# Turning the residual stream on TensorE instead of through DRAM, and scaling it earlier, in a two-block transformer kernel

## The reference

```python
def first_block(x, ...):
    ...
        h = h + jnp.einsum("bsf,fd->bsd", jax.nn.silu(gate) * val, w_down[l])
    return rms_norm(h, final_norm)

def hybrid_layer(x, norm_gain, w_in, w_out, rel_bias, cos, sin):
    hn = rms_norm_2(x, norm_gain)
    proj = hn @ w_in.astype(hn.dtype)
    ...                                  # chunked attention ya (8 heads), retention yr (4 heads)
    y = jnp.concatenate([ya * jax.nn.silu(ag), yr * jax.nn.silu(rg)], axis=-1)
    return x + y @ w_out.astype(x.dtype)

def second_block(x, positions, norm_gain, w_in, w_out, rel_bias, final_gain):
    cos, sin = rotary_tables(positions, RET_HEAD_DIM)
    for layer in range(DEPTH_2):
        x = hybrid_layer(x, norm_gain[layer], w_in[layer], w_out[layer], rel_bias[layer], cos, sin)
    return rms_norm_2(x, final_gain)
```

## Time and profile before

| | us |
|---|---|
| median of 3 runs (1199.81 to 1199.93) | 1199.88 |
| the profiled execution | 1199.93 |
| its span | 1198.1 |
| PE busy | 1187.1 |
| DVE busy | 868.2 |
| ACT busy | 582.3 |
| POOL busy | 286.3 |

### The profile page before, as it was taken

How to read it: one execution, slowest core, us unless ns; L and a number is a source line. 1 busy time by engine, 2 the same in 40 slices (tenths; PEclk the granted TensorE clock), 3 DMA queues, 4 the chain that set the end, 5 groups by cost and what they waited for, 6 DMA issues and landing times.

```text
span 1198.1 us, 15692 instructions
## 1 busy us (share of the span) xinstructions
PE 1187.1 (99%) x5869; PEld 1007.4 (84%) x5869; DVE 868.2 (72%) x1433; ACT 582.3 (49%) x1040; POOL 286.3 (24%) x299
## 2 busy tenths in 40 slices
PE   8999999999999999999999999999999999999998
PEld 7888888888888888888888889889888889899886
DVE  6789755555776487547776788898847788988746
ACT  6666433333443244325444477754445477754542
POOL 0220399921100000000004511266322311012300
PEclk9999999999999999999999999999999999999999
DMA  6421333333331533243333366752223376663621
GB/s 187 132 80 57 97 103 88 105 89 106 124 92 53 153 89 105 72 123 88 105 89 89 105 193 185 201 160 71 71 71 106 96 212 192 179 174 115 159 71 71
DMA packets 213009, 139.53 MB, mean 116 GB/s; under 512 B 5610, under 2 KB 204740, under 8 KB 212804
## 3 DMA queue, kind: packets, MB, share of 16 engines
q1 hardware_dynamic: 212932, 138.52, 39.9%
HBM read 123.82 MB, written 14.68 MB: 116 GB/s over the span
## 4 chain that ended last, share of the span: by engine, by line
PE 94%; DVE 2%; ACT 2%; DMA 1%; issue 1%; SPq 0%; POOL 0%; DVEq 0%; ACTq 0%
PE ps L191 93%; PE ps L194 1%; DMA xtm<-in_x_dram 1%; DVE b_pt L164 1%; ACT whi L161 0%; ACT b_p L161 0%; DVE tmp L164 0%; DMA raw<-in_w_in_dram 0%; DVE b_pd L182 0%; DVE wlo L164 0%; SPq L197 0%; DVE xtm L178 0%; ACT x1l L161 0%; ACT h L161 0%; DVE stat L167 0%
## 5 line engine op out<-in xcount | busy, mean ns | idle before, releaser
L161 ACT ACTIVATE whi<-raw 128x1024 fp32r<-128x1024 f32 (+1 forms) x198 | 206.6, 1051 | 306.1 <-PE ps L191 295.4
L164 DVE TENSOR_TENSOR wlo<-raw,whi 128x1024 fp32r<-128x1024 f32 (+1 forms) x192 | 246.1, 1288 | 48.4 <-ACT whi L161 47.8
L191 PE MATMUL ps<-x0l,whi 128*128 128x512 f32 x1008 | 255.3, 391 | 0.0
L191 PE MATMUL ps<-x0h,whi 128*128 128x512 f32 x1008 | 255.0, 391 | 0.0
L191 PE MATMUL ps<-x0h,wlo 128*128 128x512 f32 x1008 | 253.9, 390 | 0.0
L191 PEld LDWEIGHTS ps<-x0h,wlo 128*128 128x128 f32 x1008 | 188.5, 188 | 38.8
L191 PEld LDWEIGHTS ps<-x0l,whi 128*128 128x128 f32 x1008 | 187.8, 188 | 38.1
L191 PEld LDWEIGHTS ps<-x0h,whi 128*128 128x128 f32 x1008 | 187.5, 188 | 37.9
L164 POOL TENSOR_TENSOR sums<-sums,sq 128x512 f32<-128x512 f32 x28 | 43.6, 1569 | 423.2 <-ACT sq L161 423.2
L191 PE MATMUL ps<-x1h,wlo 128*128 128x512 f32 x304 | 82.3, 389 | 0.0
L191 PE MATMUL ps<-x1h,whi 128*128 128x512 f32 x304 | 82.3, 389 | 0.0
(11 more groups left out here) (190 smaller groups left out, 1671.8 us busy)
## 6 DMA issues: line engine op xcount, KB each, us to landing
raw<-in_w_in_dram SPq DMA_DIRECT2D x98, 512.0 KB, 4.1
raw<-in_w_up_dram SPq DMA_DIRECT2D x44, 512.0 KB, 3.8
raw<-in_w_out_dram SPq DMA_DIRECT2D x24, 512.0 KB, 4.1
turned<-b_pd SPq DMA_DIRECT2D x16, 640.0 KB, 3.2
raw<-in_w_down_dram SPq DMA_DIRECT2D x16, 512.0 KB, 4.1
b_px<-turned SPq DMA_DIRECT2D x32, 160.0 KB, 3.7
b_p<-turned SPq DMA_DIRECT2D x32, 160.0 KB, 3.6
raw<-in_w_down_dram SPq DMA_DIRECT2D x8, 384.0 KB, 3.5
```

The costliest lines, as they stand in the source:

```text
L161: return AC.put(lambda e: e.activation(o, i, func, **kw), after, AC, 1)
L164: return on.put(lambda e: e.tensor_tensor(o, a, b, op), after, on, 1)
L191: return PE.put(lambda e: e.matmul(o, l, r, start=start, stop=stop), after, PE if mark else None, 1)
```

## The change

`h_final` is gone. Its 16 POOL instructions are issued inside `norm_steps` for layer 0, right behind the spread of RB2, so that they stand at the start of the layer. `h_turn` now uses four PE transposes of 128x128 into bank 6 and an ACT copy back into Hk(k) one step later, at steps 64, 66, 68, 74, 76, 78, 80 and 85 of layer 1. `h_back`, the DRAM tensor and its semaphores are gone. The additions at the end read H as (feature block, token block, 128) instead of in runs of 32.

```diff
-        def norm_steps(eps, n=1, wait=1):
+        def norm_steps(eps, n=1, wait=1, rb2_free=None):
...
                 if n == 2:
-                    rb["rb2"] = spread(RB2[:, :], r[:, 0:16], t)
+                    t2 = spread(RB2[:, :], r[:, 0:16], t)
+                    for k in range(8):
+                        t = tt(Hk(k), Hk(k), RB2[:, :], ALU.mult, after=[t2, h_read[k]], on=PO)
+                        h_tok[k] = ts(Hk(k), Hk(k), FIN(k), None, ALU.mult, after=t, on=PO)
+                    rb2_free.append(t)
...
-            st, steps = norm_steps(1e-5, 2, 3) if l == 0 else norm_steps(1e-6)
+            st, steps = norm_steps(1e-5, 2, 3, slot_free[5]) if l == 0 else norm_steps(1e-6)
...
-            def h_final(k):
-
-                t = tt(Hk(k), Hk(k), RB2[:, :], ALU.mult, after=[rb["rb2"], h_read[k]], on=PO)
-                h_tok[k] = ts(Hk(k), Hk(k), FIN(k), None, ALU.mult, after=t, on=PO)
-                slot_free[5].append(t)
-                yield
...
             def h_turn(k):
 
-                pd = PD[:, 512 * (k % 2):512 * (k % 2) + 512]
-                t = blocks(pd.rearrange("p (i t c) -> p i t c", i=4, t=4),
-                           Hk(k).rearrange("p (t i c) -> p i t c", t=4, i=4), after=[h_tok[k], pd_free[0], turn_free[k % 2]])
-                turn_free[k % 2] = [dma(HT[128 * k:128 * k + 128, :], pd, d_ht[k % 2], after=t)]
-                h_read[k].append(t)
-                yield
-
-            def h_back(i):
-
-                src = HT.rearrange("(x j) (i c) -> i j x c", x=32, i=4)[i]
-                h_back_tok.append(dma(H[32 * i:32 * i + 32, :].rearrange("p (x c) -> p x c", c=128), src, d_hb,
-                                      after=[turn_free, [h_read[k] for k in range(8)]]))
-                yield
+                free = claim(6)
+                for t in range(4):
+                    tp = tr(PS[6][:, 128 * t:128 * t + 128], H[:, 512 * k + 128 * t:512 * k + 128 * t + 128], IDENT,
+                            after=[h_tok[k], free], mark=t == 3)
+                yield 1
+                h_tok[k] = act(Hk(k), PS[6][:, :], after=[tp, h_read[k]])
+                bank_free[6] = [h_tok[k]]
...
-            if l == 0:
-                for k in range(8):
-                    at_step(49 + 3 * k, h_final(k))
-            else:
-                for k in range(8):
-                    at_step(63 + 2 * k, h_turn(k))
-                for i in range(4):
-                    at_step(81 + 2 * i, h_back(i))
+            if l == 1:
+                for k, n in enumerate((64, 66, 68, 74, 76, 78, 80, 85)):
+                    at_step(n, h_turn(k))
...
-        hv = H[:, :].rearrange("p (x t c) -> p x t c", t=4, c=32)
-        small = lambda a: a.rearrange("p (x c) -> p x c", c=32)
+        hv = H[:, :].rearrange("p (k t c) -> p k t c", k=8, c=128)
...
-            a = stt(small(o), small(PS[bank][:, :]), 0.5, hv[:, 0:16, t, :], ALU.mult, ALU.add, after=[tok, h_back_tok])
+            a = stt(tiles(o), tiles(PS[bank][:, :]), 0.5, hv[:, 0:4, t, :], ALU.mult, ALU.add,
+                    after=[tok, list(h_tok.values())])
```

More of the change, by code:

```diff
@@ L428, in block_then_hybrid_layers @@
         d_po = Counter(sem("s_po"))
-        d_ht = [Counter(sem(f"s_ht{i}")) for i in range(2)]
-        d_hb = Counter(sem("s_hb"))
         d_out = Counter(sem("s_out"))
@@ L1092, in block_then_hybrid_layers @@
         AT_K = [0, 4, 7, 9]
-        turn_free, h_back_tok = [[], []], []
-        HT = nc.dram_tensor("h_turned", (1024, 512), F32).ap()
         pd_free, spot_free = [[]], [[], []]
@@ L1553, in out_part @@
             o = ob[:, t, a:b]
-            x_ = stt(small(o), small(PS[bank][:, 0:n]), 0.5, hv[:, a // 32:b // 32, t, :], ALU.mult, ALU.add, after=tok)
+            x_ = stt(tiles(o), tiles(PS[bank][:, 0:n]), 0.5, hv[:, a // 128:b // 128, t, :], ALU.mult, ALU.add, after=tok)
             bank_free[bank] = [x_]
```

## The result

The changed kernel takes 1208.48 us (median of 4 runs, 1207.38 to 1208.96) against 1199.91 for the kernel before (4 runs, 1199.81 to 1200.03). The ratio is 1.0068, 95% interval [1.0054, 1.0084]: slower by 8.6 us. The forecast was 1206.0 in a range of 1202.0 to 1211.0.

A forecast was written before the change was run, and what follows sets the result against it. The prediction took TensorE as the bound: 1199.9 + 3.5 (transposes) + 0.1 (copies) + 3.5 (new pause) - 0.9 (old pause) = 1206.1, said as 1206.0 us, range 1202.0 to 1211.0.

The forecast's parts named there:

- The bound and the frame: Whole kernel: TensorE bounds it; work added to PE is paid in full, work taken from DVE, ACT or queues gains nothing.
- The transposes: Layer 1: eight groups of four PE transposes at 0.46 us, less two shared bubbles, add 3.5 us (2.8 to 3.7).
- The copies: Layer 1: PE's second transpose group waits 0.1 us for ACT's copy of the first (0 to 1 us).
- The old pause: Layer 0: PE's 0.86 us pause for b_pt at 801.30 goes, -0.9 us (-1.2 to 0).
- The new pause: Layer 0: moved scaling makes PE wait for b_pt at about 721, 3.5 us (0 to 9).
- The queue of POOL: Layer 0: the 16 instructions end at 716.9, head 2's bias at 721.2; PE pauses 3.0 us for b_pt.
- the scores of head 0: Layer 0 at 693.65: claimed safe, with 2.4 us to spare against 1.8 of lengthened b_sets.
- DVE's own lengthening: Layer 0, 684.6 to 718.8: 20 two-input operations lengthen 0.36 us each; 2.5 us left after deductions, at b_pt.
- Absorbed: Rival in layer 0: new pause only 0 to 2 us, 1202.6 to 1204.6 in all; chance 0.25.
- Alternation: Rival in layer 0: DVE operations each wait half a POOL instruction, 9.0 us, 1211.6 in all; chance 0.1.
- ACT late: Rival: an ACT copy waits behind POOL, 1 to 2 us more in any case; included in the forecast's 0.5 chance.
- Not slower: Rival: no new pause, short pauses go, groups cost 0.35 us without bubble; 1201.5 in all; chance 0.11.

The follow-up runs named there:

- no_turn: Kernel before without layer 1's turning of H (eight DVE transposes and twelve DMAs left out): 1200.24 us against 1200.30, ratio 1.0001.
- turn_twice: Kernel before with H turned on TensorE, each of the eight groups of four transposes issued twice: 1206.78 us, ratio 1.0037 to 1.0067 (1.0052) to before.
- scale_only: Kernel before with only the scaling of H moved to the start of layer 0: 1204.81 us, ratio 1.0032, 4.2 us slower.
- turn_only: Changed kernel with the scaling of H back at its old steps, so only the turning differs from before: 1204.17 us, ratio 1.0031, 3.5 us slower.
- after_fill: Changed kernel plus 12 needless 128x512 matmuls on TensorE ahead of the scores of head 2 in layer 0: 1206.06 us.
- scale_four: Kernel before with four of the eight pieces of H scaled at the start of layer 0, four at their old steps: 1199.96 us, ratio 0.9997.
- pool_writes: Kernel before plus 52 memsets of 128x512 on GpSimd, ahead of rc and rs at the start of layer 0: 1202.48 us, ratio 1.0023.
- scale_six: Kernel before with six of the eight pieces of H scaled at the start of layer 0, two at their old steps: 1202.33 us, ratio 1.0011.
- after_again: The changed kernel, unchanged, run again beside others on the same chip: 1208.34 us (4 runs, 1207.83 to 1208.88).

## Why the prediction was right, point by point

**The bound and the frame.** Right. What was added to PE's list was paid in full (3.5 us), and 5.6 us of DVE and twelve DMAs gave nothing (no_turn 1.0001).

**The transposes (3.5 us).** Right: 263.3 - 259.8 = 3.5 us, with 0.47 us for a group and the shared bubble where two stand together (from 1109.68 the two groups take 0.43 and 0.36). The 3.5 us also hold the wait for a copy (+0.15) and the short pause at 1124 that is gone (-0.29), so the transposes by themselves come to some 3.6. turn_twice confirms that the measured group, and not the duration of a transpose, is the price.

**The copies (0.1 us).** Right in place and size: the second group, 0.15 us. The tail is the same too, as I had put it: outb<-ps,h takes 692 ns at the median before and after.

**The old pause (-0.9 us).** Right: near 801 of before, which is 806 now, PE has none.

**The new pause (3.5 us).** Right in size, 3.57 us, wrong in its place, and the agreement is partly luck. It starts some five microseconds ahead of where I put it, and for another tile. Of the signs that I had named, b_p<-ps,b_m released by POOL and a pause for b_pt at 721 did not come. The queue of POOL did not decide: the 16 instructions took 27.8 us and not 32.3, so the bias came at 716.9 and not 721.2, earlier than the 717.22 at which DVE wanted it before. DVE's own lengthening did it, and at the scores of head 2, which I never checked. I had tested the scores of head 0 (693.65) and found 2.4 us to spare against 1.8, and that held, PE took them at 693.25 without a wait. The scores of head 2 depend on the first of two b_sets, here in the DVE and the PE timeline of before:

```profile
715.18 1.40 DVE L164 TENSOR_TENSOR b_sets<-tmp,b_sets 64x512 fp32r<-64x512 f32 x2
...
716.17 1.43 PE L191 MATMUL ps<-b_sets 128*128 128x512 f32 x8
```

It was over at 715.9, and PE came at 716.17: 0.3 us to spare, less than at the two consumers that I had looked at (2.4 and 0.9), and the lateness has had 30 us to add up. The group of four b_sets alone lost 2.5 us, the two wlo at 694 1.3 us, the group of six 1.7 us: 5.5 us, where I had 6.0 for the whole list. Then two errors met. I let DVE's waits absorb 2.6 us, and they shrank only from 2.55 to 1.81, by 0.7; other operations ran shorter (the first wlo took 1.37 us, and 2.03 beside rc and rs before). In the end the two b_sets began 3.5 us later than before (718.67 against 715.18) and PE came 0.4 us earlier; less the 0.3 us of lead that is the pause. The 0.9 us that I subtracted as b_pt's slack was that of the wrong consumer. With the right lead and the right absorption my sum for DVE's operations would have come to 5.0 us; the 3.5 us were my choice between the larger of two estimates (3.0 and 2.5) for another wait and their sum.

**What was not in the sum: the clock.** I put it at nothing and gave no reason, though the trace of before has the case. At its start PE waits 1.81 us for x and, from 10.2 on, 0.41 us again, and its clock is at 0.50 from 10.6 to 13.8; timeline and windows of before:

```profile
9.07 1.09 PE L194 MATMUL ps<-ca,xtm 128*128 128x128 f32 x8 [1.81 <-DMA xtm<-in_x_dram]
...
8.00:12.00 4.00, 2.52 (x15) 0.81 1.12 338
12.00:16.00 4.00, 4.00 (x20) 0.76 0.92 233
```

A pause of 3.6 us in layer 0 was followed by 3 to 6 us of work at half clock, 1.4 to 2.9 us of cost. Had I had it, the forecast would have been near 1208, and not 1206.0 against the 1208.5 measured. The stretches of the profiled execution give 1199.9 - 0.4 (start) + 3.57 + 2.6 - 0.86 + 3.5 = 1208.3, and it took 1208.31; but the 2.6 is what remained of the same stretches, so this is book-keeping and no test of the parts. scale_only, turn_only and after_fill are the tests.

**The rivals.** *Absorbed*: no. *Alternation*: in kind yes, b_sets at 1060 instead of 685 ns is 0.37 us an operation, a quarter of a GpSimd instruction and not half of one. The mean hides much: the group of four b_sets lost 0.61 us each and the two wlo at 694 0.64, while the wlo at 701.78 and 707.67 lost 0.0 and 0.1 with POOL reading all the time. What decides between them is open. *ACT late*: 0.15 us. *Not slower*: no, the bubble is there.

## What to carry to other kernels

When a block of work moves along one engine's list, go through every consumer on the bounding engine in the window in which it will run, and compare the lateness that has added up by then with the lead of that consumer; the nearest one need not be the one that fails. Where the matrix engine is the bound, price a wait of some microseconds at more than its length, as the clock may fall behind it: here 3.6 us of waiting cost 1.4 to 2.9 us more, and dummy matmuls in the gap won 2.3 us. Look for such a fall in the trace that you already have, at the start too. And before trading DMA or vector work for matrix work, take the old work out once: if the time stays, it was free.

## What the runs showed of the hardware

- PE's clock against its pauses at the start of layer 0, in the traced executions: standing for 0.86, 0.95, 1.86 and 1.95 us left it at 1.00 (after_fill, scale_four, pool_writes, scale_six); 3.57 to 3.60 us was followed by 0.50, 1.2 GHz, in all three traces that have it (after, after_again, scale_only), for 3 to 6 us of uninterrupted matmuls.
- The length of the pause alone does not decide: at the start of before, 1.81 us of standing and 0.41 us soon behind it were followed by 0.50 from 10.6 to 13.8; in layer 0 of scale_six 1.95 us was not.
- 27 us of memsets on GpSimd left wlo on DVE at 1220 ns; 28 us of instructions that read SBUF made it 1474 ns, and a 64x512 tensor_tensor 1060 instead of 685 ns.
- A 128x128 f32 transpose on PE adds 0.10 to 0.11 us in a row of them, though its record is 0.27 us long.
